# In-projection of a two-layer streaming encoder: seven block products in place of eight for nine pairs of weight chunks

## The reference

```python
h = rmsnorm(x, norm_g) * (1.0 + scale[:, None]) + shift[:, None]
z = h @ w_in                                   # 1024 -> 2752 columns
(cv_h, cv_b, cv_c, cv_g, m_q, m_kv, m_kr, m_g, s_q, s_k, s_v, s_g) = split(z)
cy, conv_state = causal_conv3(cv_c * cv_h, buf, conv_w)
out_conv = cv_b * cy * silu(cv_g)              # short convolution
out_mla = mla_attention(...) * silu(m_g)       # latent attention, 4 heads
out_swa = sink_attention(...) * silu(s_g)      # local attention in a band of 128
x = x + gate[:, None] * (concatenate([out_conv, out_mla, out_swa], -1) @ w_out)
```

## Time and profile before

| | |
|---|---|
| median of 3 runs | 1176.69 us (1176.63 to 1176.9) |
| span of the profiled execution | 1175.6 us |
| TensorE matmuls busy | 97%, 7228 instructions |
| VectorE, ScalarE, GpSimd busy | 53%, 39%, 5% |
| time of the profiled execution itself | not recorded apart; the span is 1.1 us under the median |
| DMA | 107.72 MB, mean 92 GB/s |

### The profile page before, as it was taken

How to read it: one execution, slowest core, us unless ns; L and a number is a source line. 1 busy time by engine, 2 the same in 40 slices (tenths; PEclk the granted TensorE clock), 3 DMA queues, 4 the chain that set the end, 5 groups by cost and what they waited for, 6 DMA issues and landing times.

```text
span 1175.6 us, 18014 instructions
## 1 busy us (share of the span) xinstructions
PE 1146.1 (97%) x7228; PEld 1027.2 (87%) x7228; DVE 621.4 (53%) x1067; ACT 463.8 (39%) x840; POOL 60.8 (5%) x46
## 2 busy tenths in 40 slices
PE   6999999999999999999999999999999999999996
PEld 5899999999996676699999999999999666769996
DVE  5943313337368875662485233333654888666135
ACT  4742332322256543451365223422224756455122
POOL 2000001000000000002120000100000000000211
PEclk9999999999999999999999999999999999999998
DMA  9622111111224452482131111111112351116003
GB/s 343 248 76 60 47 36 52 37 37 32 67 86 167 139 156 78 124 314 88 41 112 51 62 36 42 51 44 47 46 27 83 129 183 45 46 36 233 1 33 130
DMA packets 68798, 107.72 MB, mean 92 GB/s; under 512 B 3953, under 2 KB 59377, under 8 KB 66417
## 3 DMA queue, kind: packets, MB, share of 16 engines
q1 hardware_dynamic: 68720, 106.67, 27.1%
HBM read 93.91 MB, written 11.70 MB: 90 GB/s over the span
## 4 chain that ended last, share of the span: by engine, by line
PE 88%; DVE 6%; ACT 3%; DMA 1%; SPq 1%; issue 1%; POOLq 0%; ACTq 0%; DVEq 0%
PE psum L949 58%; PE psum L1357 6%; PE psum L1411 5%; PE psum L1391 3%; PE psum L940 1%; DVE h_lo L1978 1%; ACT rot L1617 1%; PE psum L1430 1%; PE psum L1345 1%; DMA raw<-in_w_in 1%; PE psum L1308 1%; PE psum L1344 1%; DVE w_lo L2087 1%; PE psum L1193 1%; PE psum L1367 1%; PE psum L1372 1%
## 5 line engine op out<-in xcount | busy, mean ns | idle before, releaser
L949 PE MATMUL psum<-h_hi,w_hi 128*128 128x384 f32 x1392 | 472.4, 339 | 2.7 <-DVE x L2088 1.7
L949 PE MATMUL psum<-h_lo,w_hi 128*128 128x384 f32 x1392 | 465.3, 334 | 0.0
L949 PE MATMUL psum<-h_hi,w_lo 128*128 128x384 f32 x1392 | 465.2, 334 | 0.0
L949 PEld LDWEIGHTS psum<-h_hi,w_hi 128*128 128x128 f32 x1392 | 261.3, 188 | 9.0 <-issue 7.5
L949 PEld LDWEIGHTS psum<-h_hi,w_lo 128*128 128x128 f32 x1392 | 261.5, 188 | 0.5 <-issue 0.5
L949 PEld LDWEIGHTS psum<-h_lo,w_hi 128*128 128x128 f32 x1392 | 261.3, 188 | 0.0
L2087 DVE TENSOR_TENSOR w_lo<-raw,w_hi 128x1024 fp32r<-128x1024 f32 x61 | 77.3, 1267 | 185.4 <-ACT w_hi L1612 184.8
L1612 ACT ACTIVATE w_hi<-raw 128x1024 fp32r<-128x1024 f32 (+1 forms) x62 | 65.3, 1054 | 225.7 <-PE psum L949 142.6
L1411 PE MATMUL psum<-pT,ckv 128*128 128x512 f32 x144 | 74.0, 599 | 0.8 <-ACT oL_s L1766 0.8
L1677 ACT ACTIVATE probs_p<-psum,nmax 128x128 f32<-128x128 f32 (+1 forms) x72 | 25.2, 362 | 118.1 <-DVE esink L2087 118.1
L2088 DVE SCALAR_TENSOR_TENSOR x<-psum,mod,x 128x768 f32<-128x768 f32 (+1 forms) x32 | 24.0, 751 | 67.9 <-PE psum L949 67.2
(11 more groups left out here) (255 smaller groups left out, 1461.3 us busy)
## 6 DMA issues: line engine op xcount, KB each, us to landing
raw<-in_w_in SPq DMA_DIRECT2D x18, 1024.0 KB, 5.4
raw<-in_w_mod SPq DMA_DIRECT2D x15, 1024.0 KB, 5.1
first_mod<-in_w_mod_first SPq DMA_DIRECT2D x8, 1024.0 KB, 15.3
raw<-in_w_out SPq DMA_DIRECT2D x10, 768.0 KB, 5.2
tab<-in_c_rope SPq DMA_DIRECT2D x6, 1152.0 KB, 5.2
x<-in_xT SPq DMA_DIRECT2D x3, 1536.0 KB, 9.6
...
```

The lines of the kernel that those rows point to most:

```text
L949: mm = pe.matmul(psum[:, bank, 0:BLK], w_[:, k, :], h[:, k, blk(n)], start=(k == 0 and i == 0), stop=(k == KD - 1 and i == 2))
```

## The change

**Arithmetic.** For nine pairs (all but KV_KR and Q_LAT, which stay whole) the product of token blocks 0 and 1 with the two chunks is split into halves of the contraction: A11, A12 are the slices 0 to 3 and 4 to 7 of block 0, A21, A22 those of block 1; B11, B21 are the halves of the first chunk's weights, B12, B22 of the second's. Block products number seven in place of eight (Winograd's form). A piece of weights of 4 slices by 128 columns is a **unit**:

- T3 = B22 - B12 by S3 = A11 - A21, into bank 1 (P7)
- B11 by A11, into bank 0 (P1), and by block 2, into bank 2
- B21 by block 2, then by A12, into bank 0 (P2)
- T2 = B22 - T1 by S2 = S1 - A11, into bank 4 (P6)
- T1 = B12 - B11 by S1 = A21 + A22, into bank 3 (P5)
- T4 = B21 - T2 by A22, into bank 1 (P4)
- B22 by S4 = A12 - S2, into bank 3 (P3), and by block 2, into bank 5; B12 by block 2, into bank 5

Each product is 12 matmuls (4 slices x 3, `area_products`, at L1197). Block 2 is computed as before. ScalarE copies P1 to `p16` (`first_product`), and VectorE combines: `whole_0` gives block 0 of the first chunk, `share_6` and `share_5` add P6, P7 and P5, `whole_1` and `whole_3` give the rest (seven sums of 384 columns).

**Who does what.** S1 to S4 are made once per layer by VectorE (four sums of 1536 columns), rounded by ScalarE, with VectorE's remainders. T1 to T4 are made for each pair by GpSimd (`weight_sum`). The eight units of a pair go through a ring of four slots (unit w in slot w % 4), where each is rounded by ScalarE (`unit_split`) and its remainder taken by VectorE (`unit_rest`). TensorE says when it has done with a unit (u_used).

**Order.** The pairs come as KV_KR, Q_LAT, M_G0, M_G1, S_Q, SK_SV, S_G, CV_H, CV_C, CV_B, CV_G. The latents' squares and turns move to SK_SV, local attention begins in S_G (`with_local`), two tiles to a pair. VectorE's work on a chunk is cut in two: `take` reads PSUM and frees the banks, `work` does the rest (second half of a rope, the convolution, the last gating). What was L949 is L1061 for the whole pairs and the out-projection.

**Memory.** The latent gates are kept in a tile of their own, stored to DRAM by two DMAs and loaded into `mix[:, 2:6]` after the last unit is used. The rope table of the second layer is loaded later in the out-projection; some weight slots and small tiles move.

```diff
-KV_KR, Q_LAT, SK_SV, S_Q, S_G, M_G0, M_G1, CV_H, CV_C, CV_B, CV_G = range(11)
-PAIRS = [(1280, 192), (1024, 256), (2240, 256), (1984, 256), (2496, 256), (1472, 256), (1728, 256),
+KV_KR, Q_LAT, M_G0, M_G1, S_Q, SK_SV, S_G, CV_H, CV_C, CV_B, CV_G = range(11)
+PAIRS = [(1280, 192), (1024, 256), (1472, 256), (1728, 256), (1984, 256), (2240, 256), (2496, 256),
          (0, 256), (512, 256), (256, 256), (768, 256)]
 NIN, NOUT = 2 * len(PAIRS), KD
+WHOLE = 2
+NWHOLE = 2 * WHOLE
+SEVENS = len(PAIRS) - WHOLE
+T3, B11, B21, T2, T1, T4, B22, B12 = range(8)
+UNITS = 8
+RING_SLOTS = 4
+S3, S1, S2, S4 = range(4)
...
+                def weight_sum(p, u):
+                    n = UNITS * (p - WHOLE)
+                    if u == T3:
+                        s, count, _ = unit_view(p, B22, last)
+                        pool.wait_ge(w_in[s].sem, w_in[s].at(lane.layer, count))
+                        if n:
+                            pool.wait_ge(u_used.sem, u_used.at(lane.layer, n - UNITS + T1 + 1))
+                        else:
+                            pool.wait_ge(z_done.sem, z_done.at(lane.layer, 2 * Q_LAT + 1))
+                    elif u == T1:
+                        pool.wait_ge(u_used.sem, u_used.at(lane.layer, n + T3 + 1))
+                    elif u == T2:
+                        if n:
+                            pool.wait_ge(u_used.sem, u_used.at(lane.layer, n))
+                        else:
+                            pool.wait_ge(z_done.sem, z_done.at(lane.layer, 2 * Q_LAT + 2))
+                    else:
+                        pool.wait_ge(u_used.sem, u_used.at(lane.layer, n + B11 + 1))
+                    of = lambda b: unit_view(p, b, last)[2]
+                    a, b = {T3: lambda: (of(B22), of(B12)), T1: lambda: (of(B12), of(B11)),
+                            T2: lambda: (of(B22), as_unit(p, unit_sum[T1 % RING_SLOTS])),
+                            T4: lambda: (of(B21), as_unit(p, unit_sum[T2 % RING_SLOTS]))}[u]()
+                    lane.link(pool.tensor_tensor(as_unit(p, unit_sum[u % RING_SLOTS]), a, b, ALU.subtract), w_sum)
...
+                weight_sum(WHOLE, T3)
+                for p in range(WHOLE, len(PAIRS)):
+                    weight_sum(p, T1)
+                    weight_sum(p, T2)
+                    weight_sum(p, T4)
+                    if p == WHOLE:
+                        pool.wait_ge(z_act.sem, z_act.at(lane.layer, Q_SQUARED))
+                        pool.tensor_tensor(mix[:, 1, :], mix[:, 1, :], mix[:, 7, :], ALU.add).then_inc(lat_acc.sem, 1)
+                    if p + 1 < len(PAIRS):
+                        weight_sum(p + 1, T3)
+                    if p == SK_SV:
+                        for i in range(2):
+                            latent_root(i)
...
+                def seven(p, then):
...
+                    pe.wait_ge(z_dve.sem, z_dve.at(lane.layer, 2 * p - 1))
+                    unit(T3)
+                    area_products(T3, summed(S3), 1, True, True).then_inc(u_used.sem, 1)
+                    then("T3")
+                    unit(B11)
+                    area_products(B11, plain(0, 0), 0, True, True).then_inc(p1_mm.sem, 1)
+                    then("P1")
+                    area_products(B11, plain(0, 2), 2, True, False).then_inc(u_used.sem, 1)
+                    then("B11")
+                    unit(B21)
+                    area_products(B21, plain(1, 2), 2, False, True)
+                    then("block 2")
+                    pe.wait_ge(p1_c.sem, p1_c.at(lane.layer, n + 1))
+                    area_products(B21, plain(1, 0), 0, True, True).then_inc(u_used.sem, 1)
+                    then("B21")
+                    pe.wait_ge(z_dve.sem, z_dve.at(lane.layer, 2 * p))
+                    unit(T2)
+                    area_products(T2, summed(S2), 4, True, True).then_inc(u_used.sem, 1)
+                    then("T2")
+                    unit(T1)
+                    area_products(T1, summed(S1), 3, True, True).then_inc(u_used.sem, 1)
+                    then("T1")
+                    unit(T4)
+                    pe.wait_ge(shared.sem, shared.at(lane.layer, 2 * n + 1))
+                    area_products(T4, plain(1, 1), 1, True, True).then_inc(u_used.sem, 1)
+                    then("T4")
+                    unit(B22)
+                    pe.wait_ge(shared.sem, shared.at(lane.layer, 2 * n + 2))
+                    area_products(B22, summed(S4), 3, True, True)
+                    then("P3")
+                    area_products(B22, plain(1, 2), 5, True, False).then_inc(u_used.sem, 1)
+                    then("B22")
+                    unit(B12)
+                    area_products(B12, plain(0, 2), 5, False, True).then_inc(u_used.sem, 1)
+                    then("B12")
...
+                def with_local(t):
+                    def then(after):
+                        if t == 0 and after in ("T3", "P1", "B11"):
+                            turn_values(("T3", "P1", "B11").index(after))
+                        elif after == "P1":
+                            local_turn(t - 1)
+                        elif after == "block 2":
+                            if t:
+                                local_weigh(t - 1)
+                            local_scores(t)
+                        elif after == "T1":
+                            local_turn(t)
+                        elif after == "P3":
+                            local_weigh(t)
+                            if t < ST:
+                                local_scores(t + 1)
+                            else:
+                                turned(0)
+                        elif after == "B22" and t == ST:
+                            turned(1)
+                            turned(2)
...
+                def whole_0(p):
+                    used(p, B21)
+                    dve.wait_ge(p1_c.sem, p1_c.at(lane.layer, p - WHOLE + 1))
+                    tt(bank(0), p16[:], bank(0), ALU.add)
+                def share_6(p):
+                    used(p, T2)
+                    tt(p16[:], p16[:], bank(4), ALU.add)
+                    tt(p167[:], p16[:], bank(1), ALU.add, sig=shared)
+                def share_5(p):
+                    used(p, T1)
+                    tt(bank(4), p167[:], bank(3), ALU.add)
+                    tt(p16[:], p16[:], bank(3), ALU.add, sig=shared)
...
+                for p in range(WHOLE, len(PAIRS)):
+                    t = 2 * (p - S_G)
+                    if p > WHOLE:
+                        take(2 * p - 1)
+                        if p == SK_SV + 1:
+                            query_norm()
+                        work(2 * p - 1)
+                        if p == S_G + 1:
+                            local_gate(0)
+                    unit_rest(p, T2)
+                    unit_rest(p, T1)
+                    unit_rest(p, T4)
+                    if p == WHOLE:
+                        sum_rest(S4)
+                    if t >= 0:
+                        if t:
+                            local_gate(t - 1)
+                        local_maxima(t)
+                    whole_0(p)
+                    if t >= 0:
+                        local_normalise(t)
+                    share_6(p)
+                    unit_rest(p, B22)
...
+                    unit_rest(p, B12)
+                    share_5(p)
...
+                    whole_1(p)
...
+                    unit_rest(p + 1, T3)
+                    unit_rest(p + 1, B11)
...
+                    take(2 * p)
+                    if 0 < t < ST:
+                        local_gate(t)
+                    if 0 <= t < ST:
                         local_maxima(t + 1)
+                    whole_3(p)
+                    unit_rest(p + 1, B21)
+                    if 0 <= t < ST:
                         local_normalise(t + 1)
+                    work(2 * p)
...
+                sp.wait_ge(u_used.sem, u_used.at(lane.layer, UNITS * SEVENS))
+                sp.wait_ge(mg_out.sem, mg_out.at(lane.layer, 32))
+                sp.dma_start(mix[:, 2:6, :], mg_kept).then_inc(mg_in.sem, 16)
```

579 lines of the change are left out of this document (392 added, 187 removed).

## The result

The changed kernel takes **1196.01 us** (median of four runs, 1194.65 to 1196.62) against 1176.8: 1.6% slower, ratio 1.016 (95% interval 1.0146 to 1.0175). The forecast had the sign and 7.6 of the 19.2 us; the time lies above its range. The profiled execution took 1196.62, its span 1194.6.

A forecast was written before the change was run, and what follows sets the result against it. TensorE, busy 97%, was taken to bound the kernel. Removed matmuls save 37.4 us, waits add 22.5 per layer, 45.0 in all: 7.6 us slower, 1184.3 us by the median; range 1160 to 1192.

The forecast's parts named there:

- M_G0: First pair of seven products: GpSimd's addition of squares and late remainders and sums make TensorE wait 2.8 us per layer.
- S_Q, SK_SV, S_G: Pairs with rotations and latents: waits for bank 1, the latents, the values' turn and S_G's P3, together 5.2 us per layer.
- CV_H, CV_C, CV_G: Local-attention pairs: VectorE's chain before P3 takes 13.6 us against TensorE's 12.2; 1.4, 1.4 and 1.3, together 4.1 per layer.
- CV_B: Convolution pair: VectorE's queue costs 6.5 us, GpSimd's sums holding up the convolution 3 x 1.3; together 10.4 per layer.
- The values' turn: After S_G's first unit work, the values' turn waits 2.5 us per layer for VectorE's rope rest, take and query norm.
- the bank: S_Q to SK_SV: rotation starts behind two roundings, so the take that frees bank 1 ends 1.2 us late per layer.
- the latents: S_Q to SK_SV: the latents' squares and means, now behind unit work, cost 1.2 us per layer.
- S_G's P3: S_G's own third product waits 0.3 us per layer.
- Rival 3: After CV_B's wait the clock falls too: 2 us lost per layer, 1188 us, up to 1194; chance 0.09.
- the upper case: CV_B: GpSimd's T1, T2 and T4 sums hold up the convolution, 3 x 1.3 us per layer; lower bound 0.
- Rivals 1 and 2: 1: VectorE and GpSimd hardly meet, 1166.9 us, chance 0.26; 2: waits are covered, 5 us per layer, 1149, chance 0.10.
- GpSimd wins the hand-over: Where VectorE and GpSimd contend for SBUF, a waiting GpSimd goes first; used for the late case in the local pairs.

The follow-up runs named there:

- the reordered kernel: Changed kernel plus GpSimd's latent addition later, P5's sums before B12's remainder, convolution cut in pieces, ropes and latents' chain reordered: 1147.79 us, ratio 0.9746.
- filler in CV_B: Changed kernel plus 32 matmuls, result overwritten, on TensorE in CV_B before its wait for T2's remainder: 1199.45 us, ratio 1.0187.
- filler before the values: Changed kernel plus 22 matmuls, result overwritten, on TensorE in S_G behind T3, where it idles for the turned values: 1193.75 us, ratio 1.0135.
- the kernel with the convolution in pieces: Changed kernel with P5's sums before B12's remainder, convolutions cut at their taps and spread out, T4's remainder behind the local maxima: 1175.99 us, ratio 0.9992.

## Why the prediction was wrong

**Right.** The products are 3960 (1584 at the old loop, 2376 at the new line); a plain pair takes 23.0 us (22.9 forecast; two chunks took 24.96 before), so the 37.4 us of saving are nearly real: the reordered kernel shows 29.0 of them, and its steps of CV_B (29.1 for 26.6) and CV_G's wait (0.6) account for 6.2 of the missing 8.4. TensorE idles 20 us per layer, all but 3.0 of them in the places named, the longest time (5.8, for 7 forecast) before CV_B's T2.

Against each term, as the excess of a step over the same step without the waits (23.0 plain, 26.6 with two tiles; for S_Q to S_G the 50.9 of the reordered kernel):

| place | forecast per layer | measured |
|---|---|---|
| M_G0 | 2.8 | 3.1 (3.2) |
| S_Q, SK_SV, S_G | 5.2 | 10.2 (11.5) |
| CV_H, CV_C, CV_G | 1.4 + 1.4 + 1.3 | 1.6 + 1.6 + no wait seen |
| CV_B | 10.4 | 10.3 (10.7) |

**The step that failed** is "S_Q to SK_SV: ... Together 5.2": it is 5.0 and 6.3 short, 11.3 us, where 1184.3 and 1196.0 are 11.7 apart. (All terms together come to 55.2 us for 45.0, 17.8 net of the saving; 1.4 of the 19.2 measured lies outside the steps, and CV_G's term was 1.3 too high.) The excess is the waits of the two steps (0.9 + 1.2 + 1.8 + 3.8 = 7.7, and 7.9 in the second layer) and the clock, which the sum put at nothing (2.4 and 3.6). The first thing missing is a second wait for the same tile. The step priced one rotation behind two roundings. But S_Q has two, and both write `rot`. ScalarE's, VectorE's and GpSimd's timelines:

```profile
153.45 4.60 ACT L1795 ACTIVATE rot<-psum 32x1152 f32<-32x1152 f32 x4
...
164.68 4.59 ACT L1795 ACTIVATE rot<-psum 32x1152 f32<-32x1152 f32 x4 [5.97 <-DVE sqT L2366]
169.31 0.49 ACT L1896 ACTIVATE p<-psum 128x384 f32<-128x384 f32 x1
```

```profile
158.14 1.36 DVE L2366 TENSOR_TENSOR sqT<-psum,tab 128x1152 f32<-128x1152 f32 x1 [3.63 <-ACT rot L1795]
...
162.25 2.32 DVE L2366 TENSOR_TENSOR sqT<-sqT,rot 128x1152 f32<-128x1152 f32 x1
169.46 1.36 DVE L2366 TENSOR_TENSOR sqT<-psum,tab 128x1152 f32<-128x1152 f32 x1 [4.90 <-ACT rot L1795]
...
172.25 1.36 DVE L2366 TENSOR_TENSOR sqT<-sqT,rot 128x1152 f32<-128x1152 f32 x1
173.64 2.14 DVE L2366 TENSOR_TENSOR unit_lo<-unit_sum,unit_hi 128x512 fp32r<-128x512 f32 x3
```

```profile
162.06 1.29 POOL L902 TENSOR_TENSOR unit_sum<-raw 128x512 f32<-128x512 f32 x1 [10.03 <-PE psum L1197]
```

The second rotation starts when VectorE has read the first (164.57), and behind it stand P1's copy (TensorE waits 1.2) and the remainder of T2 (1.8): 3.0 us per layer that no term had. Of the delay 1.0 us is a meeting that the forecast passed over: the sum of the rope that reads `rot` took 2.32 beside GpSimd's sum and 1.36 without one, ten microseconds later. The values' turn waits 3.8 for the 2.5 forecast; against that the terms for the bank (1.2), the latents (1.2) and S_G's P3 (0.3) came to 0.9 in all. Sharing out the rotations and moving the ropes' second halves takes 9.5 to 10.8 us off, the clock's part included.

The second is the clock. Rival 3 had it fall after CV_B's wait, 1188 to 1194. It did fall there, and cost nothing in the first layer, since VectorE set the pace (filler in CV_B), and some 0.4 us in the second, where it stayed low for longer. It fell also twice from S_Q to S_G, where TensorE decides: 2.4 and 3.6 us together, 2.2 of them for the fall at the values' wait when it comes alone (filler before the values). What makes the earlier one, at 175 and 752 us, come or stay away is not shown. This is the rival nearest to what came, with the wrong place. The Trainium skill (TensorE: Matmul & The Clock Gate, "Part 1: The HAM clock gate") has the throttled state as the default that activity lifts: the trace agrees, 1.00 with the wait filled and 0.83 with it empty.

**The port.** That GpSimd's sums hold up the convolution was taken at its upper end, 3.9 us. VectorE's timeline in CV_B, first convolution and second:

```profile
283.25 2.89 DVE L2368 TENSOR_SCALAR mix<-u,vec 128x1024 f32<-128x1024 f32 x2
286.18 4.29 DVE L2367 SCALAR_TENSOR_TENSOR mix<-u,vec,mix 128x1024 f32<-128x1024 f32 x4
...
291.26 1.74 DVE L2366 TENSOR_TENSOR u<-psum,mix 128x768 f32<-128x768 f32 x3
293.04 1.07 DVE L2368 TENSOR_SCALAR mix<-u,vec 128x1024 f32<-128x1024 f32 x2
294.15 3.38 DVE L2367 SCALAR_TENSOR_TENSOR mix<-u,vec,mix 128x1024 f32<-128x1024 f32 x4
```

GpSimd's sums, same stretch:

```profile
283.04 1.32 POOL L902 TENSOR_TENSOR unit_sum<-raw 128x512 f32<-128x512 f32 x1 [12.03 <-PE psum L1197]
284.44 1.62 POOL L902 TENSOR_TENSOR unit_sum<-raw,unit_sum 128x512 f32<-128x512 f32 x1
287.65 1.35 POOL L902 TENSOR_TENSOR unit_sum<-raw,unit_sum 128x512 f32<-128x512 f32 x1 [1.59 <-PE psum L1197]
```

The first convolution, with three sums beside it, takes 1.82 and 0.91 us more than the second, which has none: 2.7 us for the 3.9 taken. So the convolution is held up, as the upper case had it. That CV_B's excess came to 10.3 and 10.7 for the forecast's 10.4 is partly luck: the meeting was 1.2 smaller and the wait before T2 5.8 for 7, so other parts of VectorE's queue took longer than their terms; which ones was not traced. The Trainium skill (SBUF — State Buffer, "SBUF: two separate sides") calls the port pair an exclusive lock for the whole instruction. The trace agrees, with the 2.7 us here and in M_G0, where the three remainders took 4.6 us for 2.1 while the addition ran (94.40 to 97.08). Put back alone, the addition costs 2.3 per layer.

**Rivals 1 and 2** were wrong: the meetings did not fall away, and the waits were not covered. (The forecast's "GpSimd wins the hand-over" is no rule, though: in the kernel with the convolution in pieces the one that began first won, once each.) "Only another order removes them" was right, and the order exists.
